# Regrouping the low-rank matmuls of the RWKV head group: by kind instead of by column tile

## The reference, cut to what matters

```python
r, k, v, wd, ad, gd = split_cols(u, [RW_W, RW_W, RW_W, RW_W_RANK, RW_A_RANK, RW_G_RANK])   # ranks 32, 32, 64
g = jax.nn.sigmoid(gd) @ g_up
for d in range(2):
    w = jnp.exp(-RW_DECAY_SCALE * jax.nn.sigmoid(w0[d] + jnp.tanh(wd) @ w_up[d]))
    a = jax.nn.sigmoid(a0[d] + ad @ a_up[d])
```

## Time and profile before

| | |
|---|---|
| median of 3 runs | 1188.59 us |
| lowest and highest run | 1184.58 and 1197.24 us |
| the profiled execution's own time | 1188.59 us |
| its span in the profile | 1186.7 us |
| mean granted TensorE clock over the span | 0.918 |

### The profile page before, as it was taken

The page is one execution under the profiler, slowest core; times in us unless marked ns, Lnnn a source line. Parts: engine busy times, 40 slices in busy tenths (PEclk is TensorE's granted clock), DMA queues, the critical chain, the costliest instruction groups (busy, mean ns, idle before and its releaser), DMA issues. The chain is left out here.

```text
span 1186.7 us, 23521 instructions
## 1 busy us (share of the span) xinstructions
PE 982.4 (83%) x10169; PEld 659.7 (56%) x10169; DVE 459.9 (39%) x1267; ACT 291.0 (25%) x600; POOL 86.8 (7%) x144
## 2 busy tenths in 40 slices
PE   3999989889879789775699998989888959977741
PEld 2555657688645566432445565768864546643321
DVE  1361666378431521111445075728832161111114
ACT  2431235342211411100143214543221231100100
POOL 0000000000000022112100000000000002221120
PEclk8999999899889799999599998989988979999985
DMA  9679123300266399998932121430027548999963
GB/s 385 253 183 286 50 107 143 144 4 9 76 248 243 149 360 378 365 381 311 376 124 78 64 76 71 154 134 4 8 78 301 204 170 307 376 360 383 377 227 131
DMA packets 39438, 239.55 MB, mean 202 GB/s; under 512 B 5344, under 2 KB 5344, under 8 KB 15776
## 3 DMA queue, kind: packets, MB, share of 16 engines
q1 hardware_dynamic: 26784, 194.69, 43.4%
q0 software_dynamic: 12544, 43.27, 11.6%
HBM read 210.15 MB, written 27.79 MB: 201 GB/s over the span
## 5 line engine op out<-in xcount | busy, mean ns | idle before, releaser
L925 PE MATMUL bank<-sb_hT,sb_ring 128*128 128x385 f32 (+1 forms) x640 | 213.0, 490 | 4.4 <-ACT sb_hT L1495 4.4
L925 PEld LDWEIGHTS bank<-sb_hT,sb_ring 128*128 128x128 f32 (+1 forms) x640 | 118.7, 188 | 93.7 <-issue 12.8
L925 PE MATMUL bank<-sb_ring,sb_arena 128*64 128x256 f32 (+4 forms) x776 | 113.6, 395 | 25.9 <-DMA sb_ring<-weights 13.9
L1495 ACT ACTIVATE sb_arena<-bank 128x128 f32<-128x128 f32 (+5 forms) x104 | 43.6, 433 | 298.3 <-PE bank L925 248.7
L925 PEld LDWEIGHTS bank<-sb_ring,sb_arena 128*64 128x64 f32 (+2 forms) x776 | 70.0, 153 | 64.5 <-issue 23.6
L925 PE MATMUL bank<-sb_arena 64*64 64x64 f32 (+5 forms) x960 | 90.6, 331 | 14.7 <-DMA sb_arena<-weights 11.2
L1495 ACT ACTIVATE sb_u<-bank 128x256 f32<-128x256 f32 (+4 forms) x98 | 44.7, 467 | 211.7 <-PE bank L925 210.2
L925 PE MATMUL bank<-sb_o,sb_ring 128*128 128x385 f32 x256 | 89.5, 513 | 8.0 <-issue 8.0
L1795 DVE TENSOR_TENSOR sb_arena<-sb_arena,bank 128x128 f32<-128x128 f32 x67 | 17.9, 286 | 181.2 <-ACT sb_arena L1495 174.8
L925 PE MATMUL bank<-sb_u,sb_arena 64*64 64x64 f32 (+2 forms) x824 | 74.1, 326 | 14.8 <-DMA sb_u<-weights 10.3
L925 PE MATMUL bank<-sb_ring,sb_scond 128*32 128x128 f32 x1536 | 60.8, 321 | 26.5 <-DMA sb_ring<-weights 23.7
(11 more groups left out here) (201 smaller groups left out, 1215.2 us busy)
## 6 DMA issues: line engine op xcount, KB each, us to landing
sb_ring<-weights SPq DMA_DIRECT2D x115, 1024.0 KB, 8.3
sb_arena<-weights SPq DMA_DIRECT2D x30, 1024.0 KB, 21.3
sb_u<-weights SPq DMA_DIRECT2D x24, 1024.0 KB, 19.4
y_slots<-sb_arena POOLq DMA_DIRECT2D x70, 128.0 KB, 6.7
x_slots<-sb_o POOLq DMA_DIRECT2D x1, 6912.0 KB, 39.8
sb_sq<-weights SPq DMA_DIRECT2D x6, 1024.0 KB, 16.5
sb_hT<-weights SPq DMA_DIRECT2D x6, 1024.0 KB, 17.0
sb_sq<-x_slots POOLq DMA_DIRECT2D x18, 256.0 KB, 7.4
```

The source lines that it names most:

```text
L925: return nc.tensor.matmul(out, lhsT, rhs, start=start, stop=stop, skip_group_check=True)
L1495: return nc.scalar.activation(out, in_, func, **kw)
```

## The change

The ten products of each layer stay the same, and so do their number of banks and the tiles that they stand behind. They are issued by kind. The first group becomes the four `wl` matmuls, the second group the four `al` matmuls and then the two `gg` matmuls. `psum_plan`, TensorE and ScalarE follow the same new order. Each matmul now opens its own bank and waits for `lora_ready` just ahead of it, where before the banks of a step were all opened first.

```diff
-AFTER_U = {2: ["lora0", "lora1"], 3: ["lora2", "lora3"], 4: ["key_squares"], 6: ["rw_values"], 8: ["bonus"],
+AFTER_U = {2: ["decay_lora"], 3: ["a_lora", "gate_lora"], 4: ["key_squares"], 6: ["rw_values"], 8: ["bonus"],
...
-                    parts = [("wl", (i // 2, i % 2), 0, 32), ("al", (i // 2, i % 2), 32, 64)]
-                    if i < 2:
-                        parts.append(("gg", (i,), 64, P))
-                    banks_ = [open_bank(pe, name, l, *key) for name, key, _, _ in parts]
-                    pe.wait_ge(lora_ready, l + 1)
-                    for bank, (_, _, r0, r1) in zip(banks_, parts):
-                        mm(bank[:, 0:W], Lp("lora", slice(r0, r1))[:, i * P:(i + 1) * P], mixed_lora[r0:r1, 0, :])\
+                def lora(name, r0, r1):
+                    for d in range(2):
+                        for i in range(2):
+                            bank = open_bank(pe, name, l, d, i)
+                            pe.wait_ge(lora_ready, l + 1)
+                            c = d * 256 + i * P
+                            mm(bank[:, 0:W], Lp("lora", slice(r0, r1))[:, c:c + P], mixed_lora[r0:r1, 0, :])\
+                                .then_inc(psum_filled, 1)
+
+                if step == "decay_lora":
+                    lora("wl", 0, 32)
+                elif step == "a_lora":
+                    lora("al", 32, 64)
+                elif step == "gate_lora":
+                    for i in range(2):
+                        bank = open_bank(pe, "gg", l, i)
+                        mm(bank[:, 0:W], Lp("lora", slice(64, P))[:, i * P:(i + 1) * P], mixed_lora[64:P, 0, :])\
                             .then_inc(psum_filled, 1)
```

More of the change, by code:

```diff
@@ L214, in psum_plan @@
             for step in AFTER_U.get(c, ()):
[L215 to L218, removed]
-                    if i < 2:
-                        g("a", "gg", l, i)
-                elif step in ("key_squares", "rw_values"):
+                if step in ("decay_lora", "a_lora"):
+                    for i in range(4):
+                        g("a", {"decay_lora": "wl", "a_lora": "al"}[step], l, i // 2, i % 2)
+                elif step in ("gate_lora", "key_squares", "rw_values"):
                     for i in range(2):
-                        g("a", {"key_squares": "kkn", "rw_values": "rvt"}[step], l, i)
+                        g("a", {"gate_lora": "gg", "key_squares": "kkn", "rw_values": "rvt"}[step], l, i)
                 elif step == "bonus":
@@ L977, in after_u @@
             def after_u(l, step):
-                if step[:4] == "lora":
-                    i = int(step[4])
-                    parts = [("wl", (i // 2, i % 2), 0, 32), ("al", (i // 2, i % 2), 32, 64)]
-                    if i < 2:
-                        parts.append(("gg", (i,), 64, P))
-                    banks_ = [open_bank(pe, name, l, *key) for name, key, _, _ in parts]
-                    pe.wait_ge(lora_ready, l + 1)
-                    for bank, (_, _, r0, r1) in zip(banks_, parts):
-                        mm(bank[:, 0:W], Lp("lora", slice(r0, r1))[:, i * P:(i + 1) * P], mixed_lora[r0:r1, 0, :])\
+                def lora(name, r0, r1):
[14 more added lines that the diff above has]
+                        mm(bank[:, 0:W], Lp("lora", slice(64, P))[:, i * P:(i + 1) * P], mixed_lora[64:P, 0, :])\
                             .then_inc(psum_filled, 1)
@@ L1563, in after_u @@
             def after_u(l, step):
[L1564 to L1570, removed]
+                if step in ("decay_lora", "a_lora"):
+                    name, out, bias = ("wl", sgw, "w0") if step == "decay_lora" else ("al", asig, "a0")
+                    for d in range(2):
+                        for i in range(2):
+                            bank = filled(act, name, l, d, i)
+                            k = 2 * d + i
+                            f(out[:, k, :], bank[:, 0:W], ACT.Sigmoid, bias=Lc(bias, k))\
+                                .then_inc(read(name, l, d, i), 1)
+                elif step == "gate_lora":
+                    for i in range(2):
                         bank = filled(act, "gg", l, i)
```

## The result

The changed kernel took 1202.17 us (median of 4 runs, 1195.44 to 1205.78) against 1186.59 us for the kernel before (4 runs, the three given above and one more). The ratio is 1.0104, 95% interval 1.0062 to 1.0147, so it is 7 to 17 us slower, most likely 12; the two medians alone stand 15.6 us apart, which such few runs do not settle. A later session with 12 runs gave 1.0080 (1.0045 to 1.0114), 9.5 us. The forecast was 4.4 us slower. The direction was right and the size was not: 1202.17 lies above the upper end of the range, 1200, and so, just, does the time of the profile of before with the 12.3 us added, 1200.9.

What follows compares the result with a forecast made beforehand. TensorE, busy throughout the input projection, was taken as the bound there. The profiled 1188.6 us plus 4.4 us of TensorE time over two layers, all other terms 0, gave 1193.0 us, range 1187 to 1200.

Steps and rivals of the forecast that it cites:

- TensorE's own time: Input projection, low-rank groups: first group 0.58 us less, second 2.80 us more, so +2.22 us per layer.
- The price of a slot and of a change of height: TensorE in the input projection: 0.324 us per slot, plus 0.2 us when the height of matmul changes.
- the rule: TensorE in the input projection: only neighbouring matmuls of the same height on different rows share a slot.
- Added waits, weight loads, ScalarE, VectorE: Input projection: already fulfilled waits and hidden loads cost 0, ScalarE keeps up, VectorE's earlier finish gains 0.
- rival (c): Input projection: weight loads on a single row group stand open, +10.5 us, 1199.1 us; 7 in 100.
- VectorE's gain: `decay_sums` scans lose their 2.92 us wait, but VectorE then only waits longer for TensorE; gain 0.
- rival (a): Input projection: VectorE's chain sets the stage and its removed wait pays, 5.8 us off, 1182.8 us; 4 in 100.
- ScalarE's wait for the key squares: Input projection: ScalarE waited 3.38 us for the key squares before; about 3 us of that stay.
- The shift arrives: End of the input projection: VectorE waits for TensorE's first scores, so the whole 2.2 us per layer go on.
- rival (b): After the input projection: a later wait swallows the 2.2 us, 1188.6 us; 6 in 100.
- The clock: TensorE's granted clock in the input projection: expected to stay at 1.00, so it added nothing to the forecast.
- rival (d): Clock halves behind the new groups, tiles 4 and 5 at half speed, 5.15 us per layer, 1203.3 us; 5 in 100.

Runs made afterwards that it cites:

- gg later: Changed kernel with the two `gg` moved from behind `al` to behind tile 5; ratio 1.0039 to the kernel before.
- long row: Kernel before with all ten low-rank matmuls by kind in one row behind tile 3 (four `wl`, four `al`, two `gg`); ratio 1.0043 to the kernel before.
- half of the rows: Changed kernel with `wl` and `al` over rows 0 to 63, half of the weights zeros; ratio 0.9980 to the kernel before.

## Why the forecast was right in direction and wrong in size

**TensorE's own time: right.** Forecast +2.22 us per layer. The groups lasted 2.78 and, with `gg` partly at the lower clock, 4.92 us (4.29 forecast); where no fall came (gg later) the stage was longer by 2.44 and 2.39 us with one more change of height, so 2.2 us without it. The price of a slot and of a change of height held in every run. What the rule lacked is that matmuls of one height on different rows also overlap at the border of two unequal groups (long row, half of the rows).

**Added waits, weight loads, ScalarE, VectorE: right.** The four `wl` stand 2.78 us, so neither the waits nor the loads stood open; rival (c) is out. (The two `gg` wait only for their banks, not for `lora_ready` as the text ahead says of each matmul; it makes no difference to the sum.) VectorE's gain was nothing; rival (a) is out. Of ScalarE's wait for the key squares I said that about 3 us stay, and it grew to 6.91: tile 3 and 4 ran late by the low clock.

**The shift arrives: right.** The first scores are 7.4 us later and VectorE waits for them as before; rival (b) is out.

**The clock: wrong.** The step that failed is the "Against" of rival (d), and with it its 5 in 100: the sum put the clock's share at nothing, and the runs show 3.3 to 5 us of it per layer, more than the 2.2 us that the sum had. I weighed it by three rows: small-tile work at full clock, the first group of before at full clock, and a fall behind idle time. None of them was the new case. The small tiles from 224 to 230 us are 64 by 64 and overlap on the array; and in the first group of before no piece on one set of rows was longer than 0.84 us. The row that was needed, four unshared matmuls of 32 rows one behind another, was not in the trace, so the range should have gone further up. The mechanism that I described under (d) is what happened, and nearly at the price that I put on it: a fall of 10.3 us per layer, 5.15 us lost, against falls of 3.4 and 6.8 us in layer 0, 10.2 together and 5.1 lost, and 6.8 or 10.2 us in layer 1, 3.4 or 5.1 lost. What (d) had wrong is the place: the falls lie on tile 3 and on `gg` and tile 4, not on tiles 4 and 5. That the direction came out right is due to the 2.2 us per layer; the larger part of the loss was not in the forecast at all. The page of the Trainium skill that I cited beside it, "TensorE: Matmul & The Clock Gate", section "HAM oscillation", speaks of idle gaps; here the clock fell with TensorE busy in every one of these stretches (6.80 of 6.80 us in the fall from 70.6 us), so the measurement decides. The Trainium skill's same page, section "Part 1: The HAM clock gate", says that the clock follows how busy TensorE has been recently. That fits if busy is read as rows in use, a reading which the runs at 32, 64 and 128 rows bear out (8 of 8 second groups fell with 32-row `al`, none over 64 or 128 rows).

**The sum.** Two layers of 2.2 us are 4.4. In layer 0 the stage grew by 7.25, 7.14 and 7.07 us in the three profiles, so the falls add 5 us there. In layer 1 it grew by 8.20, 7.22 and 7.20; of the 8.20 about 2.7 are a low clock at the start of the stage, behind the gap ahead of it, which profiles of other kernels show too, so the falls add 3.3 to 5. That makes 13 to 14 us for the two stages, against 9.5 and 12.3 by the two ratios. So up to 5 us came back elsewhere. The traces show where: from layer 0's first scores to layer 1's first tile it is 441.71 us before and 440.50, 440.86 and 441.00 in the three profiles, and from layer 1's first scores to the end 466.9 before and 464.6, 465.5 and 463.4. But over the profiles of all kernels here the same two stretches spread from 438.1 to 449.0 and from 459.2 to 467.1 us, so this may well be chance; no run tells.

**What stays open.** Why the same row of 2.8 us brings the clock down in half of the cases. In the profiles the fall begins within 0.7 us behind such a row or not at all, and one kernel has it in one layer and not in the other, so the place of the row in time may decide; that is not shown, since no run moved a row by a known amount. Open too is why the single long row, with more unshared matmuls in it, had less low clock (3.4 and 6.8 us a layer) than the two groups of the changed kernel.

## What to carry to other kernels

Where TensorE has no idle time, count a group of small matmuls in slots, not in matmuls: neighbours on different rows of the array share a slot, neighbours on the same rows don't, and each change of height costs 0.2 us here. Then ask how much of the array is in use in the longest unshared row, since most of the price of a low clock is paid by the full-size matmuls behind it, which no diff of the small ones shows. If small matmuls can't be paired, padding them with zeros to 64 or 128 rows was the cheapest here, with no loss that the runs could tell from before; spreading them cost 4.6 us, and so did, within 1 us, the single long row and the kernel with `gg` later, both of which had falls. The changed kernel cost 10 to 12.

## What the runs showed of the hardware that I had not expected

- The granted clock can fall to half with TensorE busy without a gap: 8 of 8 times in groups of four unshared 32-row matmuls with two of 64 rows, 0 of 8 groups when the rows in use were raised to 64 or 128 with zeros.
- A zero-padded matmul over 128 rows cost less than the 32-row one that does the same work, even apart from the clock: stage +1.27 us against +2.44 (gg later), since there is no change of height.
- Matmuls of equal height on different rows overlap across the border of two groups: 12 passes in 2.89 us, where 12 slots of 0.324 us would be 3.9.
